# Gated projection and gates in high and low parts, raw tiles ahead of query rows, and six rounds of the last choosing in attention steps 17 to 22

## The reference

```python
x += 0.5 * swiglu(rms_norm(x), w_ffn1)
h = rms_norm(x)
a, b, q, k, v, qi, ki, wi, gc, ga = split(h @ w_in)
u = a * sigmoid(b)                       # a, b: 512 channels each
conv = silu(layer_norm(depthwise_conv31(u))) @ w_cout
q, k = rope(rms_norm(q)), rope(rms_norm(k))
keys = top_k(index_scores(qi, wi, ki))   # 128 of the prompt, 256 of 4104 cached
att = softmax(q . k[keys]) @ v[keys]     # 8 heads x 64
x += (sigmoid(gc) * conv + sigmoid(ga) * (att @ w_aout)) @ w_o
x += 0.5 * swiglu(rms_norm(x), w_ffn2)
```

## Time and profile before

| | us |
|---|---|
| median of three runs | 1585.39 |
| lowest, highest | 1580.94, 1587.18 |
| profiled execution | 1588.44 |
| its span | 1586.6 |
| PE, DVE busy in it | 1484.6 (94%), 1104.5 (70%) |
| ACT, POOL busy | 499.6 (31%), 585.4 (37%) |
| mean granted TensorE clock | 0.977 of full |

### The profile page before, as it was taken

The page is one execution under the profiler, slowest core; times in us unless marked ns, Lnnn a source line. Parts: engine busy times, 40 slices in busy tenths (PEclk is TensorE's granted clock), DMA queues, the critical chain, the costliest instruction groups (busy, mean ns, idle before and its releaser), DMA issues. The chain is left out here.

```text
span 1586.6 us, 20793 instructions
## 1 busy us (share of the span) xinstructions
PE 1484.6 (94%) x8219; PEld 1147.5 (72%) x8219; DVE 1104.5 (70%) x1680; ACT 499.6 (31%) x756; POOL 585.4 (37%) x412
## 2 busy tenths in 40 slices
PE   5989999899999989999899789999999999999998
PEld 2323488677888865446666445669999999999998
DVE  1357399999985898999996676565679865565221
ACT  2233322112112222121212344464346544453221
POOL 2001264443338865554245775013120645520000
PEclk9998999999999999999999898999999999999999
DMA  9994153222226888868458776023422332222222
GB/s 343 389 381 161 50 85 113 93 80 80 80 80 221 286 276 276 290 213 278 125 163 269 222 237 187 17 101 126 138 75 68 93 107 82 92 68 74 74 87 93
DMA packets 156931, 248.77 MB, mean 157 GB/s; under 512 B 11965, under 2 KB 104909, under 8 KB 156571
## 3 DMA queue, kind: packets, MB, share of 16 engines
q1 hardware_dynamic: 131742, 164.22, 32.0%
q0 software_dynamic: 23104, 76.16, 15.4%
q10 hardware_dynamic: 1989, 7.07, 1.1%
HBM read 237.58 MB, written 10.20 MB: 156 GB/s over the span
## 5 line engine op out<-in xcount | busy, mean ns | idle before, releaser
L2651 POOL TENSOR_TENSOR w_lo<-w_raw,w_hi 128x1024 fp32r<-128x1024 f32 x65 | 165.5, 2546 | 294.8 <-ACT w_hi L1303 294.6
L686 PE MATMUL ps<-bh,wqr 128*128 128x288 f32 x936 | 205.3, 295 | 4.2 <-DVE wqr L1843 2.0
L1303 ACT ACTIVATE w_hi<-w_raw 128x1024 fp32r<-128x1024 f32 x88 | 91.5, 1040 | 314.7 <-PE ps L637 231.5
L2707 POOL DMA_INDIRECT kv<-cache_k,idxT x128 | 142.2, 1111 | 81.4 <-DVE kprod L2356 48.9
L2719 POOL DMA_INDIRECT kv<-cache_v,idxT x128 | 134.7, 1052 | 99.3 <-PE ps L1094 47.0
L686 PEld LDWEIGHTS ps<-bh,wqr 128*128 128x128 f32 x936 | 155.5, 188 | 5.0 <-DVE wqr L1843 3.9
L637 PE MATMUL ps<-h_hi,w_hi 128*128 128x512 f32 x352 | 139.2, 395 | 2.8 <-POOL w_lo L2651 1.5
L637 PE MATMUL ps<-h_lo,w_hi 128*128 128x512 f32 x352 | 137.7, 391 | 0.0
L637 PE MATMUL ps<-h_hi,w_lo 128*128 128x512 f32 x352 | 137.7, 391 | 0.0
L1079 PE MATMUL ps<-h,wn 128*128 128x288 f32 x448 | 115.5, 417 | 8.1 <-ACT sgb L1587 4.6
L702 PE MATMUL ps<-a_hi,wqr 128*128 128x288 f32 x704 | 122.3, 295 | 0.0
(11 more groups left out here) (493 smaller groups left out, 3268.9 us busy)
## 6 DMA issues: line engine op xcount, KB each, us to landing
w_raw<-w_ffn_in SPq DMA_DIRECT2D x56, 512.0 KB, 13.1
wq<-w_ffn_in SPq DMA_DIRECT2D x40, 512.0 KB, 3.6
wn<-w_in SPq DMA_DIRECT2D x36, 512.0 KB
qb<-q_scratch SPq DMA_DIRECT2D x64, 256.0 KB
ring<-w_ffn_in SPq DMA_DIRECT2D x28, 512.0 KB
w_raw<-w_ffn_out SPq DMA_DIRECT2D x24, 512.0 KB, 10.1
wq<-w_ffn_out SPq DMA_DIRECT2D x20, 512.0 KB
ring<-w_ffn_out SPq DMA_DIRECT2D x14, 512.0 KB
```

Of the source, the lines that this page charges most:

```text
L686: mm = pe.matmul(ps[:, bank + m, 0:HALF], w[:, k, m * P:(m + 1) * P], b[:, j, k, :], start=(j in (0, 1, 5) and k == 0 and fst), stop=(k == ...
L1303: act.activation(w_hi[:, slot, 0:n], w_raw[:, slot, 0:n], ACT.Copy).then_inc(S_("hi_ready"), 1)
L2651: pool.tensor_tensor(w_lo[:, slot, 0:n], w_raw[:, slot, 0:n], w_hi[:, slot, 0:n].bitcast(F32), ALU.subtract)\
L2707: pool.indirect_dma_start(kv[:, n % KV, c, :], None, rows[0], bass.IndirectOffsetOnAxis(ap=idxT[:, c, n:n + 1], axis=0))\
```

## The change

- The 24 mixed and gate tiles become units UA to UA + 23 of the split form; the merge products move to UM = UA + 24. `mix_unit` calls `unit`, `gate_half` does three products. ScalarE makes the high parts. GpSimd makes the low parts of units 0 to 9 and 11, VectorE those of 10, 12 to 15 and, in the steps after those in `HI_AT`, 16 to 23.
- h has to be in two parts too: ScalarE copies h32 to x_hi between the relus, VectorE subtracts it in place to h_lo ahead of the late keys. x_hi lies where xT is, so SP writes xT to DRAM (8 x 295 KB) among the native loads and reads it back among the loads of the merge.
- SP: raw tiles have two slots and are loaded ahead of the last query rows; the prompt's k and v go out after the load of unit 14 instead of unit 18's.
- prompt_qk: ScalarE squares q and k, VectorE sums with one reduction. The rope needs no copy at the end. The softmax of the sample: no subtraction over L, eight exponentials with bias and sum on ScalarE in place of one exponential and a sum on VectorE. The probabilities are turned after mixed unit 7 instead of 6. `u_pair(1)` stands before `choose(1, 7, 16)`.
- `choose(3, 10, 16)` moves from before the steps into steps 17 to 22, one round each.
- GpSimd's gathers of values 0 to 2 no longer wait for mixed unit 2, and stand between low parts.
- Semaphore counts are moved to fit (x_moved, h_ready, hhi_ready, exp_ready).

```diff
--- before.py
+++ after.py
...
+        (x_hi,), _ = place(used["xT"][0], [("x_hi", (P, KD, NT), F32R)])
+        (qk_sq,), _ = place(used["qTp"][0], [("qk_sq", (P, 4, DA), F32)])
+        x_dram = nc.dram_tensor("x_scratch", (P, KD, NT), F32, kind="Internal").ap()
...
+        HI_AT = {3: 16, 5: 17, 9: 18, 11: 19, 15: 20, 17: 21, 21: 22, 25: 23}
...
-                queries(UA + m)
+                if m < 13:
+                    queries(UA + m)
...
             for g, (col, n) in enumerate(((COL_I, NI), (COL_Q, DA), (COL_K, DA), (COL_V, DA))):
...
+                    if 4 * g + j == 6:
+                        sp.wait_ge(S_("iTp_ready"), 1)
+                        sp.wait_ge(S_("ping_free"), 17)
+                        sp.wait_ge(S_("pong_free"), 17)
+                    for k in {6: (0, 1, 2), 7: (3, 4, 5), 8: (6, 7)}.get(4 * g + j, ()):
+                        sp.dma_start(x_dram[:, k, :], xT[:, k, :]).then_inc(S_("x_moved"), 16)
...
-                native_load(m, win_v[:, 4 * (m % 2):4 * (m % 2) + 4, col:col + 256], 1024)
+                if m < NB + 2:
+                    sp.wait_ge(S_("ring_used"), N_RING + (11, 14)[m - NB])
+                load(UA + m - NB, win_v[:, 4 * (m % 2):4 * (m % 2) + 4, col:col + 256], m % 2, 1024)
+                while m < NB + 4 and sent[0] < (55, 57, 60, NS)[m - NB]:
+                    query_load(sent[0])
+                    sent[0] += 1
...
-                if n == 10:
+                if n == 6:
...
                     for b in range(4):
...
-            sp.wait_ge(S_("ring_used"), N_RING + 35)
...
-            sp.wait_ge(S_("ring_used"), N_RING + 38)
...
-            sp.wait_ge(S_("ring_used"), N_RING + NATIVE)
+            sp.wait_ge(S_("unit_used"), UM - 1 + 3)
...
                 sp.wait_ge(S_("gate_saved"), 16 * (i + 6))
...
             load(UM + 2, va[:, :, 512:768], 0, 1024)
...
+                for k in (2 * i, 2 * i + 1):
+                    sp.dma_start(xT[:, k, :], x_dram[:, k, :]).then_inc(S_("x_moved"), 16)
                 load(UM + 4 + i, vc[:, :, 256 * i:256 * i + 256], i % 2, 1024)
...
             def mix_unit(n, between=None):
...
-                if n == 0:
-                    pe.wait_ge(S_("hf_ready"), 2 * KD)
+                if n < 2:
+                    pe.wait_ge(S_("h_ready"), KD + 4 * n + 4)
...
-                pe.wait_ge(S_(f"ring{(NB + n) % RING}"), native_count(NB + n))
...
-                mm.then_inc(S_("ring_used"), 1)
+                unit(UA + n, n % 2, x_hi, h_lo, 4 * (n % 2), 4, half, n % 2 == 0, n % 2 == 1, between)
...
-                if n == 6:
+                if n == 7:
...
             def gate_half(n, m):
...
-                    pe.wait_ge(S_(f"ring{(NB + n) % RING}"), native_count(NB + n))
+                    pe.wait_ge(S_("lo_ready"), UA + n + 3)
...
+                hi = w_hi[:, n % 2, :].rearrange("p (k n) -> p k n", k=4)
+                lo = w_lo[:, n % 2, :].rearrange("p (k n) -> p k n", k=4)
...
+                    for w, x, fst in ((hi, x_hi, True), (hi, h_lo, False), (lo, x_hi, False)):
+                        for hf_ in range(2):
+                            mm = pe.matmul(ps[:, 2 * m + hf_, 0:HALF], w[:, k, m * P:(m + 1) * P],
+                                           x[:, 4 * (n % 2) + k, hf_ * HALF:(hf_ + 1) * HALF],
+                                           start=(n % 2 == 0 and k == 0 and fst), stop=(n % 2 == 1 and k == 3 and w is lo))
...
-                    mm.then_inc(S_("ring_used"), 1)
+                    mm.then_inc(S_("unit_used"), 1)
...
+                    act.wait_ge(S_("nat_evac"), 8)
+                    act.activation(qk_sq[:, :, :], qn[:, :, :], ACT.Square).then_inc(S_("nat_squares"), 1)
...
                         relu(8 * j, 8 * j + 8)
+                        if j < 2:
+                            act.wait_ge(S_("x_moved"), 64 + 16 * KD)
+                            for k in range(4 * j, 4 * j + 4):
+                                act.wait_ge(S_("hf_ready"), KD + k + 1)
+                                act.activation(x_hi[:, k, :], h32[:, k, :], ACT.Copy).then_inc(S_("hhi_ready"), 1)
...
+                if g == 3:
+                    act.wait_ge(S_("ring_used"), N_RING + 12)
+                    hi(UA)
                 for b in range(4):
+                    if g == 3 and b == 3:
+                        act.wait_ge(S_("ring_used"), N_RING + 15)
+                        hi(UA + 1)
...
+            hi(UA + 2)
+            hi(UA + 3)
             for pr in range(2):
-                act.wait_ge(S_("ring_used"), N_RING + NB + 4 * pr + 2)
+                act.wait_ge(S_("unit_used"), UA + 4 * pr + 1 + 3)
...
                 sigmoid(0)
...
                     qk_root(0)
+                    for n in (4, 5, 6):
+                        hi(UA + n)
+            hi(UA + 7)
...
-            act.activation(L[:, :, :], L[:, :, :], ACT.Exp, scale=HD ** -0.5).then_inc(S_("exp_ready"), 1)
+            for h in range(H):
+                act.activation(L[:, h, :], L[:, h, :], ACT.Exp, scale=HD ** -0.5, bias=small[0:NS, 40 + h:41 + h],
+                               accum_out=small[0:NS, 50 + h:51 + h]).then_inc(S_("exp_ready"), 1)
+            hi(UA + 8)
+            hi(UA + 9)
...
             fill(1)
...
+            act.activation(qk_sq[:, :, :], kn[:, :, :], ACT.Square).then_inc(S_("nat_squares"), 1)
...
+            hi(UA + 10)
...
-                act.wait_ge(S_("ring_used"), N_RING + NG + 2 * i + 2)
+                act.wait_ge(S_("unit_used"), UA + 2 * i + 9 + 3)
...
                 sigmoid(0)
+                hi(UA + 2 * i + 11)
                 save_gate(i)
...
+                    hi(UA + 12)
...
+                    hi(UA + 14)
...
+                if i in HI_AT:
+                    hi(UA + HI_AT[i])
...
             def rope(x1, x2, o1, o2, cos, sin, a, b):
-                link(dve.tensor_tensor(a, x1, cos, ALU.mult))
-                lk(dve.tensor_tensor(b, x2, sin, ALU.mult))
-                lk(dve.tensor_tensor(a, a, b, ALU.subtract))
...
-                link(dve.tensor_tensor(b, x1, sin, ALU.mult))
+                link(dve.tensor_tensor(a, x2, sin, ALU.mult))
+                lk(dve.tensor_tensor(b, x1, sin, ALU.mult))
+                link(dve.tensor_tensor(x1, x1, cos, ALU.mult))
...
-                link(dve.tensor_tensor(o2, b, x2, ALU.add))
-                lk(dve.tensor_copy(o1, a))
+                link(dve.tensor_tensor(o1, x1, a, ALU.subtract))
...
+                dve.wait_ge(S_("nat_squares"), w + 1)
...
-                qk_squares(v, rt1[:, :, :, :].rearrange("p b h d -> p (b h) d"), msq, rt2[:, 0, 0:1, :].rearrange("p a b -> p (a b)"))\
-                    .then_inc(S_("ms_ready"), 1)
+                lk(dve.tensor_reduce(msq, qk_sq[:, :, :].rearrange("p b (h d) -> p (b h) d", d=HD), AX.X, ALU.add))
+                dve.tensor_scalar(msq, msq, 1.0 / HD, EPS, ALU.mult, ALU.add).then_inc(S_("ms_ready"), 1)
...
-            late = keys_at(UA + 12, UM + NATIVE)
+            for k in range(KD):
+                dve.wait_ge(S_("hhi_ready"), KD + 1 + k + 1)
+                dve.tensor_tensor(h_lo[:, k, :], h32[:, k, :], x_hi[:, k, :].bitcast(F32), ALU.subtract).then_inc(S_("h_ready"), 1)
+            late = keys_at(UA + 12, UA + NATIVE)
...
             prompt_qk(0)
...
-            dve.tensor_tensor(L[:, :, :], L[:, :, :], mx.unsqueeze(2).to_broadcast([NS, H, TOPK_S + NS]), ALU.subtract).then_inc(S_("shift_ready"), 1)
+            dve.tensor_scalar(mx, mx, -HD ** -0.5, None, ALU.mult).then_inc(S_("shift_ready"), 1)
             choose(1, 3, 7)
-            dve.wait_ge(S_("exp_ready"), 1)
-            lk(dve.tensor_reduce(sm, L[:, :, :], AX.X, ALU.add))
+            dve.wait_ge(S_("exp_ready"), H)
...
+            u_pair(1)
...
+            def gate_lo(n):
...
+                dve.wait_ge(S_("lo_ready"), UA + n + 2)
+                split_lo(UA + n, n % 2)
...
             choose(1, 7, 16)
+            gate_lo(10)
...
-            u_pair(1)
             prompt_qk(1)
+            gate_lo(12)
...
-                dve.wait_ge(S_("pexp_ready"), n + 1)
+                dve.wait_ge(S_("exp_ready"), H + n + 1)
...
-            choose(2, 2, 16)
-            choose(3, 0, 2)
+            choose(2, 2, 8)
+            gate_lo(13)
+            choose(2, 8, 16)
             own_heads(0)
-            choose(3, 2, 16)
+            gate_lo(14)
+            choose(3, 0, 6)
+            gate_lo(15)
+            choose(3, 6, 10)
...
+                if i - 1 in HI_AT:
+                    gate_lo(HI_AT[i - 1])
+                if 17 <= i < 23:
+                    choose(3, i - 7, i - 6)
...
+                    if pr == 0 and m == 0:
+                        dve.wait_ge(S_("x_moved"), 64 + 2 * 16 * KD)
...
             while sent[0] < NS:
+                if sent[0] == 56:
+                    pool.wait_ge(S_("ring_used"), N_RING + 13)
+                    lo(UA)
+                if sent[0] == 62:
+                    pool.wait_ge(S_("ring_used"), N_RING + NB)
```

(17 more changed lines are left out.)

43 lines of the change are left out of this document (14 added, 29 removed).

## The result

The changed kernel took 1593.49 us (median of five runs, 1588.36 to 1598.72) against 1585.39: 1.0060 of the time before, 95% interval 1.0032 to 1.0088. On two more occasions its ratio was 1.0076 (1.0054 to 1.0097) and 1.0059 (1.0040 to 1.0078). So it is slower by 0.6 to 0.8%, some 10 us, and not 15 us faster.

The account below looks back on a forecast made before the run. TensorE and VectorE were taken as close to the bound, VectorE becoming it in the steps. 5.6 + 6.8 + 4.1 - 2 = 14.5, say 15 us, took the profiled 1588.44 to 1573.4, 3 over the median: forecast 1570.4, range 1552 to 1594.

Parts of the forecast that it names:

- What bounds the kernel: Stretches from 723.64 to 1008.33: TensorE (busy 134 of 145 and 118 of 134 us) and VectorE both close to the bound.
- TensorE's saving: Split form in 14 mixed units saves 20.2 us, in 20 gate halves 16.4; together 36.6 if nothing else is in the way.
- Before 723: Ahead of the mixed units: residual writes cost 2 us, between 0 and 8; h_lo costs VectorE 5.5 us.
- The first units: Mixed units up to 8: VectorE held up beside GpSimd, GpSimd's order delays unit 3 to 761.1; 1.9 us lost.
- Units 8 to 13: Mixed units up to the attention: first mask at 868.6 against 873.46, second logits at 868.8 against 874.39, 5.6 us gained.
- The six rounds: Rounds of choosing leave the chain ahead of step 0 (9.2 us) and come back in the steps beside work.
- The steps: Attention steps 2 to 23: VectorE becomes the bound, 6.8 us gained; steps 24 to 32: 4.1 us gained.
- Locks in full: Rival: all 11 GpSimd low halves hold up VectorE, 26.4 us instead of 6.0: 1591, or 1581 if half; chance 0.26.
- Raw tiles: Rival: two raw-tile slots refill too slowly, so 14 units lose 26 us against the sum: 1597; chance 0.14.
- Nothing in the way: Rival: GpSimd's order fits the slack and VectorE isn't the bound; all 36.6 us gained: 1549; chance 0.18.
- Not what it says: Rival: split products take 0.16 instead of 0.132 us, the saving vanishes: 1585 or more; no chance of its own.
- The clock: After TensorE's idle spell near 750: a slow clock costs 1.7 us; the skill's rule alone would give up to 3.

Follow-up runs that it names:

- e7: The changed kernel with three instead of four gathers for each value tile from tile 11 on: 1578.48 us against 1595.80, ratio 0.9952 to the kernel before.
- e8: The kernel before with three instead of four gathers for each value tile from tile 11 on: 1568.12 us against 1586.64, ratio 0.9890.
- e2: The changed kernel with the last six rounds of choosing put back ahead of the attention steps: ratio 1.0080 to the kernel before.
- e3: The kernel before with only the move of six rounds of choosing into attention steps 17 to 22: ratio 1.0043.
- e4: The changed kernel without GpSimd's low parts of the mixed units, the high part multiplied twice instead: ratio 0.9988 to the kernel before.
- e6: The changed kernel with a fourth product, low part by low part, in each of the 20 gate halves: ratio 1.0147 to the kernel before.

## Why the prediction was wrong, step by step

- **What bounds the kernel.** The first failure. I read TensorE and VectorE as the pair that binds in the steps and put GpSimd "just under", from four issues of 0.95 + 0.30 a tile. Two things were missing in that term. In the changed kernel four issues of 1.09 to 1.16 and their gaps take 5.6 to 5.8 us, not 5.0 to 5.3 (in the kernel before, 1.04 and 5.4); and a slot's round has the landing in it, so that a tile took 5.8 to 6.1 us. e7 and e8 show what a quarter of it was worth: 17 and 18.5 us. TensorE's saving in steps 2 to 20, thirteen gate halves of 0.82, fell on an engine that wasn't last. Behind the gathers lies the bound that I had named: in e7 VectorE is busy 91 of 95 us.
- **TensorE's saving.** Right in size: the products of unit 3 at full clock take 0.133 each. 23.4 of the 36.6 us show in its busy time. In the result nothing is left of them.
- **Before 723.** The native tiles ended 2.5 us later in the profiles of the first chip (2 forecast); h_lo 5.43 (5.5).
- **The first units.** Mechanism right, one term too small: the locks. The three in the keys cost 1.7, 0.7 and 2.6 us, 5.0 in all (3.6 taken), two in q's ropes 2.1 each (none taken), the one in k's rope 2.2 (2.4 taken). Together that is 11.4 us on VectorE's chain, where the sum had 6.0. The last key ended at 753.95 (750.4), unit 3 began at 765.17 (761.1), unit 8 at 804.15 (799.5). The rule of the Trainium skill's page "SBUF — State Buffer" (Who interferes with whom), that a VectorE instruction with two SBUF inputs contends with a GpSimd one that reads SBUF, held again: each of these products overlaps a low part of GpSimd.
- **Units 8 to 13.** The step that failed most. By the second logits 5.6 us gained were forecast (3.6 with the 2 of the stretch before 723), and 6.0 were lost in the profile. From unit 8 to the second logits 69.3 us were forecast; it took 76.2, as good as the 76.8 of before. I had tile 5 and 6 land late, but not by 1.7 and 4.5 us of TensorE's time. I had VectorE's split 13 wait for unit 11, at 839.6 and not at 846.5, and none for the high part of unit 14. ScalarE, who makes the high parts, waits for TensorE, who waits for value tiles; that is read from the rows, not tested.
- **The six rounds.** "They come back here beside work": wrong. In the changed kernel they gain nothing on the whole (e2), and in the kernel before they cost 6.7 us (e3).
- **The steps.** From the second logits to the merge 193.3 us became 188.2 in the profiles: 5 gained of 10.9 forecast. From the end of the last value gather to the merge 83.1 and 87.0 us in the profiles of before became 77.5 to 78.1, but that gather ended 6 and 9 us later on the two chips that have both. The profiles of before stood 3 and 10 us over their medians and those of the changed kernel 5 to 1 under, so that by the timed runs nothing is left of it.
- **The rivals.** *Locks in full* gave 1581 to 1591 and comes nearest in number and in engine: GpSimd's low parts are the loss (e4: 11 to 14 us, of 20 to 26 priced). Its mechanism, VectorE held up in full, is only a part of it: 11.4 of the 26.4 us. *Raw tiles*: no wait of ScalarE is named after one ahead of units 2 to 8. Ahead of unit 2 one wait has no named releaser; it held nothing up, as GpSimd came to that unit 5.7 us later. *Nothing in the way* failed: both the loss ahead of the steps and the bounds in them stood in the way. *Not what it says* failed too: the products took 0.133 us.
- **The clock.** That idle time would be followed by slow products was right: from 765.17 to 769.56 nine pairs took 4.4 us instead of 2.4, so 2.0 on top of the 14.6 (1.7 forecast). e6 doesn't test the clock: with more work for TensorE it stood at 0.92 against 0.91.

What stays open: why e3 loses at all, how the loss ahead of the first mask divides between waits of VectorE beside GpSimd's low parts and the order of queues, how much of it is the lower clock, which part of a gather sets the pace, and why chips lie 16 us apart.

## What to carry to other kernels

Before you price what an engine saves, ask which queue each stage is *delivered* by: a software gather has an issue time, a gap, a landing time and a slot's round, and the four together can set a stage whose busy shares look free. Take a few of the deliveries away as an experiment; that is cheaper than an argument over busy shares. Then look whether the gap between the two kernels closed: here both became faster and the gap stayed, so the bound of the steps alone doesn't explain the loss. And count, for each piece of work that a change gives to an in-order queue, what it must wait for there and who is queued behind: here a split that saves one engine 1.4 us put waits of 3 to 8 us with rounds, own heads and value tiles behind them.
